# Four heads in flight in the attention of block 0 of a hybrid decoder layer

## The reference, cut to what matters

```
score = where(key_pos <= query_pos, indexer_score, -inf)
_, sel = top_k(score, 256)                    # per query
logits = q . k[sel] / 8 + bias[bucket(query_pos - sel)]
p = softmax(logits);  o = p @ v[sel]
x = x + concat(o, gla) @ w_out;  x = x + swiglu(rmsnorm(x))
```

## Time and profile before

| what | value |
|---|---|
| runs | 3987.89, 3956.91, 3982.67 us; median 3982.67 |
| profiled execution | 3957.66 us, of which span 3955.8 |
| busy over the span | PE 83%, DVE 54%, ACT 45%, POOL 43% |
| chain that ended last | PE 59%, DVE 17%, issue 7%, ACT 5%, DMA 4%, POOLq 3% |
| granted TensorE clock | mean 0.905 |
| attention of block 0 | first logits 317.57 us, first projection after it 483.82 us |
| attention of blocks 1, 2, 3 | first logits near 1141, 1966 and 2893 us; ends near 1271, 2141 and 3131 us |

### The profile page before, as it was taken

One profiled execution on the slowest core, in us unless ns is written; L12 is line 12 of the kernel. 1 busy time (PEld: TensorE's weight loads), 2 busy tenths in 40 slices (PEclk: granted clock), 3 DMA queues, 4 the chain that ended last, 5 costly groups with the idle time before them and its releaser, 6 DMA issues.

```text
span 3955.8 us, 57198 instructions
## 1 busy us (share of the span) xinstructions
PE 3279.1 (83%) x19950; PEld 1835.4 (46%) x19950; DVE 2144.8 (54%) x3923; ACT 1794.8 (45%) x2668; POOL 1719.9 (43%) x1292
## 2 busy tenths in 40 slices
PE   4972597799989978899989968799879866999865
PEld 1452345244447452344476532344367742444355
DVE  3625763799115638999244658899944421100155
ACT  0332233555445336554464346554355514554355
POOL 2014202578655024676542033676621014776434
PEclk9995699899999999899999999899989867999866
DMA  2211031223321311232210301232210253232366
GB/s 85 88 32 40 4 101 40 64 90 101 88 77 44 99 37 59 75 101 83 77 65 22 94 27 54 70 106 86 79 35 1 84 164 101 90 105 84 101 195 219
DMA packets 112067, 313.08 MB, mean 79 GB/s; under 512 B 14034, under 2 KB 20514, under 8 KB 111746
## 3 DMA queue, kind: packets, MB, share of 16 engines
q1 hardware_dynamic: 111874, 310.63, 25.2%
HBM read 296.35 MB, written 14.24 MB: 79 GB/s over the span
## 4 chain that ended last, share of the span: by engine, by line
PE 59%; DVE 17%; issue 7%; ACT 5%; DMA 4%; POOLq 3%; POOL 2%; DVEq 2%; SPq 1%; ACTq 0%
PE bank L585 15%; PE bank L587 15%; PE bank L586 15%; DVE spare L1340 7%; PE bank L835 5%; PE bank L824 3%; DVE scores L1573 2%; DVE ring L1308 1%; DMA kT<-in_w_gu 1%; ACT ring L998 1%; DVE R L1627 1%; ACT bank L1138 1%; POOL H L1902 1%; PE bank L810 1%; DVE miss L1343 1%
## 5 line engine op out<-in xcount | busy, mean ns | idle before, releaser
L585 PE MATMUL bank<-H,ring 128*128 128x512 f16 (+2 forms) x2560 | 855.6, 351 | 129.4 <-POOL H L1902 78.1
L586 PE MATMUL bank<-H,ring 128*128 128x512 f16 (+2 forms) x2560 | 855.9, 351 | 0.0
L587 PE MATMUL bank<-H,ring 128*128 128x512 f16 (+2 forms) x2560 | 855.3, 351 | 0.0
L1340 DVE TENSOR_SCALAR_CACHE_REDUCE spare<-scores,cand 128x640 uint8<-128x640 f32 (+4 forms) x448 | 662.5, 1479 | 43.5 <-issue 3.6
L1750 POOL TENSOR_TENSOR ring<-raw,ring 128x1024 f16<-128x1024 f32 (+1 forms) x252 | 487.9, 1941 | 289.9 <-ACT raw L1000 284.5
L998 ACT ACTIVATE ring<-raw 128x1024 f16<-128x1024 f32 (+2 forms) x356 | 348.9, 980 | 390.3 <-PE bank L587 143.9
L585 PEld LDWEIGHTS bank<-H,ring 128*128 128x128 f16 (+1 forms) x2560 | 259.8, 102 | 393.7 <-issue 128.6
L587 PEld LDWEIGHTS bank<-H,ring 128*128 128x128 f16 (+1 forms) x2560 | 261.0, 103 | 246.9 <-issue 8.7
L586 PEld LDWEIGHTS bank<-H,ring 128*128 128x128 f16 (+1 forms) x2560 | 260.2, 102 | 243.3 <-issue 7.4
L1627 DVE CUSTOM_DVE_ANT_0 R<-bank,scores 128x512 f32<-128x512 f32 (+3 forms) x256 | 140.8, 592 | 382.7 <-PE bank L812 373.0
L585 PE MATMUL bank<-R,ring 128*128 128x512 f16 (+1 forms) x880 | 299.0, 355 | 36.7 <-POOL R L1923 25.9
(11 more groups left out here) (296 smaller groups left out, 5966.0 us busy)
## 6 DMA issues: line engine op xcount, KB each, us to landing
raw<-in_w_gu SPq DMA_DIRECT2D x132, 512.0 KB, 3.6
raw<-in_w_in SPq DMA_DIRECT2D x104, 512.0 KB, 3.6
kT<-in_w_gu SPq DMA_DIRECT2D x88, 512.0 KB, 3.8
raw<-in_w_d SPq DMA_DIRECT2D x48, 384.0 KB, 3.2
X<-in_xT SPq DMA_DIRECT2D x8, 2048.0 KB, 9.0
raw<-in_w_d SPq DMA_DIRECT2D x48, 320.0 KB, 3.3
raw<-in_w_out SPq DMA_DIRECT2D x24, 512.0 KB, 3.5
kT<-in_w_d SPq DMA_DIRECT2D x32, 384.0 KB, 3.3
```

Of the source, the lines that this page charges most:

```text
L585: mm(o, lhs[0], rhs[0], start=first, stop=False)
L586: mm(o, lhs[0], rhs[1], start=False, stop=False)
L587: return mm(o, lhs[1], rhs[0], start=False, stop=last)
L1340: v.tensor_scalar(flags[:, 0:128 * (i + 1)], row_of(i), cut_at[:, i % 4:i % 4 + 1], None, ALU.is_ge, ALU.add, accum_out=tally[:, i % 4:i % ...
```

## The change

In block 0 the units are four in flight: logits, masks and exponentials go three units ahead. `lg` and `pT` are cut into four buffers of half the size there (a unit of block 0 has at most 512 keys; four of 1024 fit where two of 2048 did). Blocks 1 to 3 keep two buffers and one ahead. For all blocks `nearm` gets four buffers and moves to the end of `R`, and its wait is for unit u-4 instead of u-2; `mx` and `nmax` get four columns, `den` and `rden` eight, and the wait of `probs` is for the scaling of unit u-8 instead of u-4. P_NORM is 20 instead of 21, again for all blocks, while `low(k)` keeps its place behind near row 24+k. In block 0 the search of tile 2 is spread over turns 0 to 12 and that of tile 3 over 13 to 20. In the diff, the loop with `ahead(b)` is TensorE's; those of ScalarE (`probs`) and VectorE (`mask`) change in the same way.

```diff
-P_SQUARE, P_SUM, P_NORM = 10, 19, 21
+P_SQUARE, P_SUM, P_NORM = 10, 19, 20
...
-        lg = cut(Rf, 0, 2, 2048)
-        pT = cut(Rf, 4096, 2, 16, 128)
-        nearm = cut(Rf, 8192, 2, 256)
+        def buffers(b):
+            return 4 if b == 0 else 2
+        def ahead(b):
+            return buffers(b) - 1
+        lgs = {n: cut(Rf, 0, n, 4096 // n) for n in (2, 4)}
+        pTs = {n: cut(Rf, 4096, n, 32 // n, 128) for n in (2, 4)}
+        nearm = cut(Rf, 10240, 4, 256)
...
-                    logits(*units[0])
+                    for u in units[:ahead(b)]:
+                        logits(*u)
                     for n, (i, h) in enumerate(units):
-                        if n + 1 < len(units):
-                            logits(*units[n + 1])
+                        if n + ahead(b) < len(units):
+                            logits(*units[n + ahead(b)])
...
                     def probs(i, h):
...
-                        if u >= 4:
-                            act.wait_ge(S("a_scaled"), u - 3)
+                        if u >= 8:
+                            act.wait_ge(S("a_scaled"), u - 7)
...
                     def copy_pT(i, h, groups):
...
-                        if u >= 2:
-                            act.wait_ge(S("a_pv"), u - 1)
+                        if u >= nb:
+                            act.wait_ge(S("a_pv"), u - nb + 1)
...
                 for i in LATE_TILES if b == 0 else []:
-                    units = range(start, HEADS * i - 1)
+                    units = range(start, HEADS * i - ahead(b))
...
-                            if n == HEADS * i - 2:
+                            if n == HEADS * i - ahead(b) - 1:
                                 end_search([i])
...
                     def mask(i, h):
...
-                        if u >= 2:
-                            pi, ph = (u - 2) // 8, (u - 2) % 8
+                        if u >= nb:
+                            pi, ph = (u - nb) // 8, (u - nb) % 8
                             dve.wait_ge(S("a_pT"), TN[pi, ph, -(-(pi + 1) // 4) - 1] + 1)
-                            dve.wait_ge(S("a_exp"), u - 1)
+                            dve.wait_ge(S("a_exp"), u - nb + 1)
...
-                            if u >= 2:
-                                pool.wait_ge(S("a_max"), u - 1)
-                            g.tensor_tensor(nearm[:, u % 2, 0:kn], Sf[:, at:at + kn],
+                            if u >= 4:
+                                pool.wait_ge(S("a_max"), u - 3)
+                            g.tensor_tensor(nearm[:, u % 4, 0:kn], Sf[:, at:at + kn],
...
-                            if P_NORM + 2 < m:
-                                low(m - P_NORM - 3)
+                            if P_NORM + 3 < m:
+                                low(m - P_NORM - 4)
```

More of the change, by code:

```diff
@@ L177, in layer @@
         top8 = sb("top8", [128, 8])
-        mx = sb("mx", [128, 2, 8])
+        mx = sb("mx", [128, 4, 8])
         seen = sb("seen", [128, 1])
-        nmax = sb("nmax", [128, 2])
+        nmax = sb("nmax", [128, 4])
         cand = sb("cand", [128, 4], I32)
@@ L183, in layer @@
         tally = sb("tally", [128, 4])
-        den = sb("den", [128, 4])
-        rden = sb("rden", [128, 4])
+        den = sb("den", [128, 8])
+        rden = sb("rden", [128, 8])
         pages = sb("pages", [1, DB * NPG], I32)
@@ L834, in values @@
                         for t in range(i + 1):
-                            last = mm(bank[5 + u % 2][:, 0:128], pT[:, u % 2, t, :], vtok[:, t, :],
+                            last = mm(bank[5 + u % 2][:, 0:128], pTs[nb][:, u % nb, t, :], vtok[:, t, :],
                                       start=(t == 0), stop=(t == i))
@@ L852, in _ @@
                     units = [(i, h) for i in tiles_of(b) for h in range(HEADS)]
-                    logits(*units[0])
+                    nb = buffers(b)
+                    for u in units[:ahead(b)]:
+                        logits(*u)
                     for n, (i, h) in enumerate(units):
-                        if n + 1 < len(units):
-                            logits(*units[n + 1])
+                        if n + ahead(b) < len(units):
+                            logits(*units[n + ahead(b)])
                         turn(i, h, slice(0, 2))
@@ L1159, in probs @@
                         act.wait_ge(S("a_max"), u + 1)
-                        if u >= 4:
-                            act.wait_ge(S("a_scaled"), u - 3)
-                        A(lg[:, u % 2, 0:128 * (i + 1)], lg[:, u % 2, 0:128 * (i + 1)], ACT.Exp,
-                          bias=nmax[:, u % 2:u % 2 + 1], accum_out=den[:, u % 4:u % 4 + 1]).then_inc(S("a_exp"), 1)
+                        if u >= 8:
+                            act.wait_ge(S("a_scaled"), u - 7)
+                        x = lgs[nb][:, u % nb, 0:128 * (i + 1)]
+                        A(x, x, ACT.Exp, bias=nmax[:, u % nb:u % nb + 1], accum_out=den[:, u % 8:u % 8 + 1]
+                          ).then_inc(S("a_exp"), 1)
                     def copy_pT(i, h, groups):
                         u = 8 * i + h
-                        if u >= 2:
-                            act.wait_ge(S("a_pv"), u - 1)
+                        if u >= nb:
+                            act.wait_ge(S("a_pv"), u - nb + 1)
                         for g in range(-(-(i + 1) // 4))[groups]:
@@ L1188, in _ @@
                     units = [(i, h) for i in tiles_of(b) for h in range(HEADS)]
-                    probs(*units[0])
+                    nb = buffers(b)
+                    for u in units[:ahead(b)]:
+                        probs(*u)
                     for n, (i, h) in enumerate(units):
                         copy_pT(i, h, slice(0, 2))
-                        if n + 1 < len(units):
-                            probs(*units[n + 1])
+                        if n + ahead(b) < len(units):
+                            probs(*units[n + ahead(b)])
                         copy_pT(i, h, slice(2, None))
@@ L1626, in mask @@
                                 m = Sf[:, at:at + kn]
-                            v.tensor_tensor_reduce(lg[:, u % 2, k0:k0 + kn], bank[n % 3][:, 0:kn], m, 1.0 / Q_SCALE, OUTSIDE,
-                                                   ALU.add, ALU.max, mx[:, u % 2, c:c + 1]).then_inc(S("a_masked"), 1)
+                            v.tensor_tensor_reduce(lgs[nb][:, u % nb, k0:k0 + kn], bank[n % 3][:, 0:kn], m,
+                                                   1.0 / Q_SCALE, OUTSIDE, ALU.add, ALU.max, mx[:, u % nb, c:c + 1]
+                                                   ).then_inc(S("a_masked"), 1)
                         dve.drain()
-                        v.tensor_reduce(nmax[:, u % 2:u % 2 + 1], mx[:, u % 2, 0:len(cs)], AX.X, ALU.max,
+                        v.tensor_reduce(nmax[:, u % nb:u % nb + 1], mx[:, u % nb, 0:len(cs)], AX.X, ALU.max,
                                         negate=True).then_inc(S("a_max"), 1)
@@ L1635, in scale @@
                         dve.wait_ge(S("a_pv"), u + 1)
-                        v.reciprocal(rden[:, u % 4:u % 4 + 1], den[:, u % 4:u % 4 + 1])
+                        v.reciprocal(rden[:, u % 8:u % 8 + 1], den[:, u % 8:u % 8 + 1])
                         if h == 0 and i >= 2:
@@ L1640, in scale @@
                         v.tensor_scalar(osb[:, i % 2, 64 * h:64 * h + 64], bank[5 + u % 2][:, 64 * (h // 4):64 * (h // 4) + 64],
-                                        rden[:, u % 4:u % 4 + 1], None, ALU.mult).then_inc(S("a_scaled"), 1)
+                                        rden[:, u % 8:u % 8 + 1], None, ALU.mult).then_inc(S("a_scaled"), 1)
                     plan = late_picks(b)
                     units = [(i, h) for i in tiles_of(b) for h in range(HEADS)]
-                    mask(*units[0])
+                    nb = buffers(b)
+                    for u in units[:ahead(b)]:
+                        mask(*u)
                     for n in range(len(units)):
-                        if n + 1 < len(units):
-                            mask(*units[n + 1])
+                        if n + ahead(b) < len(units):
+                            mask(*units[n + ahead(b)])
                         if n in WEIGHT_UNITS:
```

6 lines of the change are left out of this document (3 added, 3 removed).

## The result

Seven runs of the changed kernel have a median of 3999.22 us (3992.53 to 4001.12), and seven of the kernel before, taken with them, 3964.09 us (3956.91 to 3987.89). The ratio is 1.0073, 95% interval 1.0048 to 1.0098: slower by 0.7%, or +35.1 us between the medians. The profiled executions differ by 39.0 us (3996.69 against 3957.66). The forecast was +36 us; its 4019 stood on a median of before that three runs had put at 3982.67 and 35 later runs put at 3964.47.

A forecast was written before the change was run, and what follows sets the result against it. The prediction took VectorE to bound block 0's attention and TensorE blocks 1 to 3. It summed 19.4 (block 0) + 11.5 (root in blocks 1 to 3) + 5 (clock) = 36, on 3982.67: 4019 us, range 3977 to 4042.

The forecast's parts named there:

- Lookahead buys nothing: Block 0's attention: three heads ahead removes none of VectorE's work or waits; 0, bounds 0 and -2.2 us.
- (a): Block 0, unit 12: near row 13 comes late behind GpSimd's low half of the first mix; VectorE stalls 4.8 us.
- (b): Block 0: with P_NORM at 20, VectorE waits for the norm's root without search steps in between; 3.0 us.
- (c): Block 0's last units: low half, near row, mask and norm form a loop, 9.6 us; mix at unit 28, 2.0.
- Block 0 in all: Block 0's attention: the stalls at mix and root and the low-half loop lengthen it by 19.4 us.
- (d): Blocks 1 to 3: the earlier root wait delays unit 22's mask by 2.4, 5.4 and 3.7 us, together 11.5.
- (e): Blocks 1 to 3: TensorE runs at a lower clock after its stops; 5 us, bounds 0 and 7.
- (f): Blocks 1 to 3: four near-row buffers do not shorten the waits, as GpSimd's own program holds the rows; 0.
- TensorE stays slow: Rival: block 0's loop keeps TensorE at 1.2 GHz until the projection, and later stops cost more; 45 us, chance 0.14.
- Only block 0 pays: Rival: the early root wait is absorbed in blocks 1 to 3; only 19.4 us lost, 4002 us, chance 0.14.
- Near rows freed: Rival: four buffers shrink VectorE's near-row waits in blocks 1 to 3; at most 20.5 us faster, 3962, chance 0.08.

The follow-up runs named there:

- four heads in flight alone: Changed kernel with root at turn 21, block 0's low halves three units later and mix split at head 6: ratio 1.0001 to the kernel before, median 3966.01 us.
- root alone: Kernel before, with only the wait for the norm's root at turn 20 instead of 21 in all four blocks: ratio 1.0052, median 3981.82 us.
- root back at 21: Changed kernel with the root wait at turn 21 again in blocks 1 to 3, block 0 keeping 20: ratio 1.0042 to the kernel before, median 3981.91 us.
- mix moved: Changed kernel with GpSimd's split of the copied query at head 6 instead of 4 in block 0: ratio 1.0063 to the kernel before, median 3984.88 us.
- four near rows alone: Kernel before, with four buffers instead of two for the near mask's rows: ratio 0.9999, median 3965.91 us.
- weight split last: Kernel before, with VectorE's four weight-tile splits moved from behind the mask to the end of their turns in block 0: ratio 0.9984, median 3953.76 us.
- joint search: Kernel before, with the thresholds of tiles 2 and 3 in block 0 searched together instead of one after the other: ratio 0.9983, median 3953.01 us.
- low halves moved by two units: Changed kernel with block 0's low halves on GpSimd two units later, at unit 26+k: ratio 1.0060 to the kernel before, median 3987.68 us.
- joint search and split last: Kernel before, with tiles 2 and 3 searched together and VectorE's weight-tile splits at turn ends in block 0: ratio 0.9992, median 3952.94 us.

## Why the prediction was right

By its steps, with what the runs put in the place of each term:

- **Lookahead buys nothing** (0, bounds 0 and -2.2). Shown by the four heads in flight alone: stage 166.4, ratio 1.0001 (0.9985 to 1.0017).
- **(a) The mix at unit 12**, 4.8: measured 5.11, in the place named and with the four GpSimd instructions named.
- **(b) The root in block 0**, 3.0: VectorE waits 2.90, and the stage of the kernel with the root alone is 3.9 longer. Under-sized by 0.9, of which 0.6 is the wait for the values in the tail, grown from 2.2 to 2.8.
- **(c) The loop**, period 4.34, seven times 1.37 = 9.6, and 2.0 for the mix at unit 28. The period is 4.33, and the one turn with the mix took 6.64. The near-row waits of block 0 were to reach some 15 us and came to 19.3, since a wait of 1.72 costs a turn only 1.36. That 20 is the last value of P_NORM that runs was not tried. Taking the loop away gave 9.0, taking the mix away gave 2.4 at that unit. The 2.0 left out that the mix cost something before, too: there the norms stand 3.78 apart at that place instead of 2.97, so the change added 2.3 - 0.8 = 1.5. And the norm of 1.19 us did not run beside GpSimd's subtraction, as the prediction says, but beside its near row (463.38 to 464.11 us in the kernel before); the loop uses the short norm either way.
- **Block 0 in all**, 19.4: 20.4.
- **(d) The root in blocks 1 to 3**, 2.4, 5.4 and 3.7, together 11.5. By the shifts of the changed kernel: 3.75 - 1.35 = 2.4 in block 1, 31.27 - 25.69 = 5.6 in block 2, 35.82 - 32.46 = 3.4 in block 3, together 11.3.
- **(e) The clock behind the stops**, 5, bounds 0 and 7. The shift grows behind those stops by 1.5 (24.34 to 25.83), 1.2 (31.27 to 32.48) and 2.5 (35.82 to 38.35), together 5.2; the kernel with the root alone has the same growth, the kernel with the root back at 21 has none of it. In blocks 2 and 3 it belongs to the stops. In block 1 it comes in three kernels without the new stop as well, so there the stop is not shown to be its cause. The term was worked out from one row, and that it fits so well is luck in part.
- **(f) Four near rows**, 0: ratio 0.9999 (0.9983 to 1.0015), and the same waits.

The sum of the measured terms is 20.4 + 11.3 + 5.2 = 36.9, against 39.0 between the profiled executions. The other 2 us are in no term: 3.0 more between 502 and 1163 us and 0.7 behind 3171 us, less 1.7 by which the changed kernel was ahead at the first logits of block 0. The 3.0 are not of the change. Over the same code the shift grows by 0.1 us in the kernel with the root at 21 in blocks 1 to 3 and by 0.25 in the one with the mix moved, which have nearly all of the change; in the kernel with four near rows alone it grows by 5.1, from -1.6 to +3.5. The 35.1 between the medians, with an interval from 19 to 39 us, agrees with the forecast but cannot test its terms; the stage lengths do.

**The rivals.** "TensorE stays slow" wanted a granted clock under 0.7 at the end of block 0, at its lower level until the projection begins. It was 0.77 over the last 47.5 us. In the first turns of the loop (461 to 480 us) it was 0.68, but there it did not stay; before the projection it was at its upper level:

```profile
490.00:502.50 12.50, 7.30 (x56) 6.40 (x56) 6.55 (x26) 3.92 (x9) 3.16 (x4) 1.00 0.01 3
```

Some 8 us into the projection the clock was low for a few us all the same, and 1.7 us of the 3.0 above were lost there: the shift goes from 18.7 to 20.4 by 515 us. That is not the loop's doing: the same 1.7 us stand at the same instructions in the weight split last and in the joint search, which have no loop, and not in the kernel with the root at 21 in blocks 1 to 3, which has the whole of it. "Only block 0 pays" is refuted by two kernels: the root alone costs 16.9 us in blocks 1 to 3, and the root put back takes all of it away. "Near rows freed" is refuted by the four near rows alone and by the changed kernel itself, where the waits for near rows in blocks 1 to 3 are still 20.5 us. The forecast took a rule from the Trainium skill (SBUF — State Buffer, Who interferes with whom): a VectorE instruction with two SBUF inputs contends with a GpSimd instruction that reads SBUF. The rows of the low halves moved by two units agree: the norm at 472.09 took 1.20 us while GpSimd added up a near row, the next one at 475.06, with GpSimd idle, 0.74.

**What was off** is the base, not the change: 4019 was 3982.67 + 36, and the median that three runs gave was 18 us too high. So 4019 lies 20 us above the measured 3999.22, and only the width of the range covers it. The prediction saw that two of the three runs stood up there and kept the lower one for the range alone.

## What to carry to other kernels

When one step of a pipeline is moved ahead, every in-order engine that serves it has to be moved ahead with all that it does in between. List, per engine, what stands between two of its products and what each of those waits for: the turns of slack that the move takes are taken from each of them, and a work item whose input is made in the same turn as the consumer's closes a loop of two engines that each wait for the other. Before deepening a pipeline, ask which engine's own work fills the stage; here a cut of VectorE's waits (6.6 us of stage) and one of its work (10.5 us) did what two more heads in flight could not. And a constant that is shared by four blocks is to be changed for the block that needs it: nearly half of the loss, some 17 us, came from the three blocks that had no use for it.

## What the runs showed of the hardware

**A stretch of low clock that comes or not.** In the gated linear attention of block 1, where TensorE is busy half to three quarters of the time, it ran at or near its upper level in the kernel before, as the granted clock shows (windows as above):

```profile
604.00:620.00 16.00, 16.00 (x290) 16.00 (x288) 0.00 (x0) 6.99 (x6) 0.00 (x0) 1.00 0.06 23
620.00:636.00 16.00, 10.07 (x84) 8.67 (x81) 4.13 (x12) 2.68 (x7) 2.69 (x2) 0.89 0.00 1
636.00:652.00 16.00, 11.66 (x99) 9.84 (x97) 5.86 (x19) 2.48 (x6) 0.00 (x0) 1.00 0.00 0
652.00:668.00 16.00, 8.64 (x40) 5.47 (x40) 3.14 (x10) 5.00 (x7) 0.00 (x0) 1.00 0.00 1
```

In the profiled execution of the kernel with the weight split last, which reached this stretch 7 us earlier, it ran at the lower one, 1.2 instead of 2.4 GHz, for all of it:

```profile
604.00:620.00 16.00, 12.56 (x209) 12.11 (x206) 0.84 (x2) 3.99 (x6) 2.69 (x2) 1.00 0.00 1
620.00:636.00 16.00, 13.72 (x61) 11.27 (x60) 3.28 (x10) 1.24 (x3) 0.00 (x0) 0.51 0.00 1
636.00:652.00 16.00, 12.39 (x55) 10.18 (x55) 4.51 (x14) 1.24 (x3) 0.00 (x0) 0.50 0.00 0
652.00:668.00 16.00, 13.72 (x60) 11.39 (x59) 3.29 (x10) 1.24 (x3) 0.00 (x0) 0.50 0.00 1
```

Both come out of a projection in which TensorE was busy throughout, and then begin to wait. The shift between the two executions goes from -6.7 us (instruction by instruction, at 496 us) to +11.2 at 671 us: 17.9 us, more than the whole edit was worth, and near the 19 us between the two groups of runs above, which are of another kernel (joint search and split last). That kernel's own profiled execution, 3949.59 us, is of the lower group, and no window of 16 us there ran at the lower clock throughout. The joint search's profiled execution shows no such stretch there (the shift grows by 2.9), and the one of four heads in flight alone has one in block 2's, where the shift goes from 12.5 to 29.1 between 1421 and 1451 us; its profiled time, 3988.85, stands 23 above its median for that. That the groups of runs are this event is argued from its size: only one run of each kernel has a profile, and none of the upper group has. What decides whether the clock falls was not settled. For an engineer the use is plain: a gain of 5 to 15 us in this kernel has to be read from the length of the stage that was edited, or from many runs, and not from one profile's end.

**The norm's length is a sign of company.** 0.74 or 1.2 us for the same instruction tells whether GpSimd worked beside it. In the changed kernel's loop it was 0.74 in each turn, with GpSimd waiting: the faster instruction was the mark of the slower stage.
